# Modulation row tiles of the second layer and of the first gates, taken in pairs

## Chip, cores and metric

The kernel runs on one core of a Trainium2 chip. The metric is the device time of one execution in microseconds, median over runs.

## The reference, cut to what matters

Everything is float32 with 256 tokens of width 2048, a context of 256 more tokens, and two blocks after one another. The first block has two layers, each with a modulation that is worked out from a condition vector:

```python
cond, cond_ctx = silu(c), silu(c_ctx)
for i in range(2):
    shift, scale, gate = split(cond @ ada_w[i] + ada_b[i], 3)      # ada_w[i]: 2048 x 6144
    h  = rmsnorm(x, norm_g[i]) * (1 + scale) + shift
    shift_c, scale_c, gate_c = split(cond_ctx @ ada_w[i] + ada_b[i], 3)
    hc = rmsnorm(ctx, norm_g[i]) * (1 + scale_c) + shift_c
    # layer 0: sliding-window attention, 16 query heads of 128 in 4 groups, its gate and output product
    # layer 1: latent attention (MLA)
    x = x + gate * o
    ctx = ctx + gate_c * oc                                        # layer 0 only
```

Then the second block: pooling mixer, MLP (2048 to 8192 and back), dilated attention, MLP, each with a layer norm.

## The kernel before

**Weight tiles.** All weights come from one stream of tiles of 128 x 2048 float32 (1 MB). `Ring` (L99 on) gives each tile taken one of five slots, the one that was released first; SyncE (L1142 on) issues one transfer for each tile in this order and waits before each for the last use of the slot. A tile of a panel is "parted": ScalarE copies it to a rounded high part `whi` (L1170, three buffers), VectorE subtracts to give the low part `wlo` in place of the raw tile (L1663), and TensorE makes three products from the two. A row tile is not parted: `row_tile` (L608) runs 4 products of `condL` (32 columns) with the raw tile, at four column positions of the array, each as two float32 instructions, so 8 instructions a tile; four tiles (k = 0 to 3) make one row of 512 modulation values in PSUM bank 5 (bank 4 or 5 for gates). Their line is L614. The row is then copied by ScalarE to `arow`, and two blocks later `ada_cols` (L627) turns it into columns, which VectorE adds to the bias.

**When a tile may be parted.** At many places in TensorE's program a mark notes how far the ring stands. ScalarE and VectorE run the same marks in their own programs and part, at a mark, all tiles that it allows:

```python
def ahead(self, stand, look):                                                    # Ring, L139
    taken, now, kept = stand
    last = min(taken - 1 + look, len(self.order) - 1)
    ready = (n for n in range(last + 1) if self.before[n] is not None and self.done_at[self.before[n]] > now)
    return next(ready, last + 1) - 1, kept
```

`look` is 2 in the attention panels and the output panels. Row tiles count as places in the ring's order. The mark of a slot is made before the row tile of this slot; a row's fourth tile makes a further mark, which ScalarE uses when it copies the row (`row_kept`). The order of the parting is thereby fixed when the program is built, and each engine does its own work in program order.

**The stages that the change touches.** For i = 0 to 3 (four panel pairs) the query panel (blocks 0 to 15) and the gate panel (blocks 16 to 31) of the first layer run as 32 blocks; a block is 12 matmuls, a weight tile serves 4 blocks. After each block `swa_slot(i, blk)` (L746) runs: the mark, then the attention steps that `ATT_AT` places there, then a row tile if `(i, blk)` is in `ADA1_AT` (L214), then `ada_cols` if the row's last tile was two blocks ago. The steps of group g run in pair g + 1: in pairs 1 and 2 after blocks 0, 1, 3, 5, 6, 8, 10, 12, 13, 15, 17, 18, 20, 22, 24, 25, 27, 29, 31; in pair 3 group 2 after 0, 1, 2, 3, 5, 6, 7, 8, 10, 11, 12, 14, 15, 16, 17, 19, 20, 21, 23, and group 3 after each block from 24 to 31 and of the first output panel from 0 to 10. A step on TensorE is the scores of n (L728, bank 6), the transposes of the probabilities of n - 2 (L604, bank 4), the product with the values of n - 3 (L741, bank 7). VectorE reads the scores of n (L1833), then scales the probabilities of n - 1 (L1844); ScalarE takes the exponential of n (L1305), then copies the transposed n - 2. In pair 3 the gated output is prepared beside it: from block 20 on ScalarE makes a high part `og_hi` and VectorE a low part `og_lo` after each step.

The output panels (p = 0 to 3, 16 blocks each) have `out_slot(p, b)` (L772): mark, steps (p = 0), and a row tile of gate p where `GATE_AT` (L215) has b; at b = 14 the gate is spread over the partitions (`gate_rows`). Their block 12 needs the last of `og_lo`.

Of the kernel before, what the change touches and what calls it, by code (L numbers as in the profile page):

```python
# [50 lines left out]
def ada_tiles(layer, n):  # L51

    if layer == 0:
        return [4 * n + k for k in range(4)]
    return [88 + 16 * (n // 3) + 4 * k + 1 + n % 3 for k in range(4)]
# [155 lines left out]

ATT_AT = att_places()
Q3_TURN = (3, 23)
ADA1_AT = {(i, 4 * j + 1): (2 * i + j // 4, j % 4) for i in range(4) for j in range(8)}  # L214
GATE_AT = {1: 0, 4: 1, 8: 2, 11: 3}  # L215
KV_ORDER = [(n, k) for k in range(4) for n in range(2)]
ADA0_AT = [5, 2, 6, 3, 7]
ADA1_ORDER = [0, 4, 1, 5, 2, 6, 3, 7]
# [29 lines left out]
def program(nc, a, out):  # L248
    ring = Ring()
    psum = Banks(ring)  # L250
    with ExitStack() as ctx:
# [192 lines left out]
        def _(pe):  # L444
            mm, tr = nc.tensor.matmul, nc.tensor.transpose

            def open_bank(key, bank, parts=1):

                b, before = psum.take(key, bank, parts)
                need(pe, bank_free[b], before)  # L450
                if b in psum.beside:
                    first, n = psum.beside.pop(b)
                    pe.wait_ge(bank_free[first], n)
                return b
# [13 lines left out]
            def weight(T, parts=True):  # L468

                n = ring.take(T, parts)  # L470
                if parts:
                    pe.wait_ge(hi_done, ring.nth[n] + 1)
                else:
                    s, v = ring.landed(n)
                    pe.wait_ge(landed[s], v)
                return n
# [10 lines left out]
            def used(n, ins):  # L487

                ins.then_inc(tile_used, 1)
                tiles_used[0] += 1  # L490
                ring.used(n, (tile_used, tiles_used[0]))

            def used_with(n, key):

                b, v, _ = psum.at[key]
                ring.used(n, (bank_full[b], v))
# [111 lines left out]
            def row_tile(key, T, k, bank):  # L608

                if k == 0:  # L610
                    open_bank(key, bank)
                n = weight(T, parts=False)
                for c in range(4):
                    last = mm(PS[32 * c:32 * c + 32, bank, :], condL[:, 4 * k + c, :], raw[:, ring.place[n], c * PW:(c + 1) * PW],  # L614
                              start=(k == 0), stop=(k == 3), tile_position=(0, 32 * c))
                if k == 3:
                    psum.mark(key)
                    last.then_inc(bank_full[bank], 1)
                    used_with(n, key)
                else:  # L620
                    used(n, last)
# [5 lines left out]
            def ada_cols(layer, n, bank):  # L627

                given(("row", layer, n))
                key = ("cols", layer, n)  # L630
                b = open_bank(key, bank)
                for c in range(4):
                    last = mm(PS[:, b, 2 * c:2 * c + 2], arow[:, c * P:(c + 1) * P], selcol[:], start=True, stop=True)
                psum.mark(key)
                last.then_inc(bank_full[b], 1)

            def gate_rows(layer, s, bank, p, rows):

                pe.wait_ge(bias_in, 16 * (5 if layer else p + 1))
                given(("row", layer, 8 + p))  # L640
                b = open_bank(("gate", layer, s, p), bank)
                last = mm(PS[:, b, :], selrow[:, s, :], rows, start=True, stop=True)
                psum.mark(("gate", layer, s, p))
                last.then_inc(bank_full[b], 1)
# [38 lines left out]
            for m, (n, k) in enumerate(KV_ORDER):  # L683
                pe.wait_ge(h_ready, 4 * (k + 1))
                pe.wait_ge(hi_done, ring.nth[kv[m]] + 1)
                for t in range(4):
                    b = open_bank(("kv", n, k, t), t)
# [23 lines left out]
            def turn_heads(what, i, n):  # L711

                pe.wait_ge(qk_ready, n)
                for h in range(4):
                    turn((what, i, h), 4 + 2 * (h % 2), [QS[:, t, h * HD:(h + 1) * HD] for t in range(4)])


            def swa_step(g, n):
                if n < 16:
                    h, t = n // 4, n % 4  # L720
                    if n == 0:
                        given(("q", g, 2))
                        given(("q", g, 3))
                        for t_ in range(4 if g == 0 else 0):
                            given(("kv", 1, 3, t_))
                    b = open_bank(("s", g, n), 6)
                    keys = kT[:, g, 0:512] if t < TT else kT[:, g, 256:512]
                    last = mm(PS[:, b, 0:keys.shape[-1]], qT[:, h, t * P:(t + 1) * P], keys, start=True, stop=True)  # L728
                    psum.mark(("s", g, n))
                    last.then_inc(bank_full[b], 1)  # L730
                if 2 <= n < 18:
                    u = n - 2
                    pe.wait_ge(swa_p, 16 * g + u + 1)
                    turn(("p", g, u), 4, [Sb[:, u % 3, c * P:(c + 1) * P] for c in range(4 if u % 4 < TT else 2)])
                if 3 <= n:
                    u = n - 3
                    given(("p", g, u))
                    b = open_bank(("o", g, u), 7)
                    toks = range(4) if u % 4 < TT else range(TT, 4)
                    for c, t in enumerate(toks):  # L740
                        last = mm(PS[:, b, 0:P], V0[:, t, g * HD:(g + 1) * HD], PTb[:, u % 2, c, :],  # L741
                                  start=(c == 0), stop=(c == len(toks) - 1))
                    psum.mark(("o", g, u))
                    last.then_inc(bank_full[b], 1)

            def swa_slot(i, blk):  # L746

                psum.mark(("slot", i, blk))
                for g, n in ATT_AT.get((i, blk), ()):
                    swa_step(g, n)  # L750
                if (i, blk) == Q3_TURN:
                    turn_heads("q", 3, 20)
                if (i, blk) in ADA1_AT:
                    r, k = ADA1_AT[(i, blk)]
                    n = ADA1_ORDER[r]
                    row_tile(("row", 1, n), ada_tiles(1, n)[k], k, 5)
                if ADA1_AT.get((i, blk - 2), (0, 0))[1] == 3:
                    ada_cols(1, ADA1_ORDER[ADA1_AT[(i, blk - 2)][0]], 5)
                if i == 0 and blk == 11:
                    turn_heads("k", 0, 4)  # L760

            for i in range(4):
                rows_panel(("qp", i), swa_qg_tiles(i, 0), swa_x, (0, 1, 2, 3), slot=lambda b: swa_slot(i, b))
                cols_panel(("gp", i), swa_qg_tiles(i, 1), swa_xT, (0, 1, 2, 3), slot=lambda b: swa_slot(i, 16 + b))
                if i < 3:
                    turn_heads("q", i, 8 + 4 * i)
# [5 lines left out]
            def out_slot(p, b):  # L772

                psum.mark(("outslot", p, b))
                for g, n in ATT_AT.get((4, b), ()) if p == 0 else ():
                    swa_step(g, n)
                if b in GATE_AT:
                    row_tile(("row", 0, 8 + p), ada_tiles(0, 8 + p)[GATE_AT[b]], GATE_AT[b], 5 - p % 2)
                if b == 14:
                    for s in range(2):  # L780
                        gate_rows(0, s, 6 + s, p, gaterow[:])

            for p in range(4):
                rows_panel(("so", p), swa_out_tiles(p), og_x, (0, 1, 2, 3), slot=lambda b: out_slot(p, b),
                           before=lambda k: pe.wait_ge(og_ready, 4 * (k + 1)) if p == 0 else None)
# [377 lines left out]
        def _(act):  # L1163
# [86 lines left out]
            def row_kept(layer, n):  # L1250

                order = ADA1_ORDER if layer else [0, 4, 1] + ADA0_AT
                r = order.index(n)
                if r or layer:
                    b, v, _ = at[("cols", layer, order[r - 1]) if r else ("cols", 0, 7)]
                    act.wait_ge(bank_full[b], v)
                take(("row", layer, n), arow[:], whole)
# [38 lines left out]
            def head_kept(what, i, h, dst):  # L1296
                take((what, i, h), dst[:, h, :], whole)
# [18 lines left out]
            def swa_slot(i, blk):  # L1316
# [4 lines left out]
                if (i, blk) == Q3_TURN:  # L1321
                    for h in range(4):
                        head_kept("q", 3, h, qT)
                if ADA1_AT.get((i, blk), (0, 0))[1] == 3:
                    row_kept(1, ADA1_ORDER[ADA1_AT[(i, blk)][0]])
                if i == 0 and blk == 11:
# [1096 lines left out]
```

## Time and profile before

| | |
|---|---|
| median of 3 runs | 3592.66 us (3592.44 to 3600.66) |
| the profiled execution | time 3590.74 us, span 3588.9 us |
| TensorE busy | 3472.1 us, 97% of the span |
| VectorE, ScalarE busy | 1891.0 us (53%), 1443.8 us (40%) |
| row-tile instructions (L614) | 768 in all, 96 tiles, 103.9 us busy |
| attention panels, output panels | about 172 to 673 us, 673 to 890 us |

TensorE's busy time is that of overlapping instructions, each begun before the one before it has ended, so durations in a row don't add up; the distance between the starts of equal instructions does. A timeline merges neighbouring equal instructions to one row with their number.

### The profile page before, as it was taken

How to read it: one execution, taken by the hardware profiler on the slowest of the kernel's cores; microseconds unless marked ns; L12 is line 12 of the kernel's file. 1: busy time of each engine (PE TensorE's matmuls, PEld its weight loads, DVE VectorE, ACT ScalarE, POOL GpSimd, SP SyncE). 2: the span in 40 equal slices, each digit the busy share in tenths (PEclk: the TensorE clock that was granted, in tenths of full speed). 3: DMA queues.
4: the chain of work that ended last, by engine and by line, in shares of the span. 5: the costliest groups of instructions: out<-in, count | busy, mean ns of one | idle time of the engine just before them, and what ended most of it. 6: DMA issues, size and time to landing. Idle time of an engine off the chain costs nothing.

```text
span 3588.9 us, 43519 instructions
## 1 busy us (share of the span) xinstructions
PE 3472.1 (97%) x18351; PEld 2850.3 (79%) x18351; DVE 1891.0 (53%) x2640; ACT 1443.8 (40%) x1612; POOL 142.8 (4%) x82
## 2 busy tenths in 40 slices
PE   7999999999999999999999999999999899999997
PEld 4677777776877668878888888878997788888886
DVE  3544455533666645457544554464445675445545
ACT  4213333422554443535433443343434444334432
POOL 0000000000000000005000000040000050000000
PEclk9999999999999999999999999999999999999999
DMA  9543333354332265454555555545543455555553
GB/s 367 224 168 137 130 130 121 115 211 164 114 112 83 106 255 182 169 206 164 211 190 197 188 188 188 189 170 188 176 153 141 164 188 211 190 197 188 188 189 127
DMA packets 90782, 626.07 MB, mean 174 GB/s; under 512 B 10326, under 2 KB 11351, under 8 KB 17755
## 3 DMA queue, kind: packets, MB, share of 16 engines
q1 hardware_dynamic: 85472, 606.72, 46.8%
q10 hardware_dynamic: 5116, 16.57, 1.2%
q8 instruction: 145, 2.38, 0.3%
q14 instruction: 49, 0.40, 0.0%
HBM read 621.15 MB, written 2.10 MB: 174 GB/s over the span
## 4 chain that ended last, share of the span: by engine, by line
PE 92%; DVE 4%; ACT 2%; issue 1%; DMA 1%; SPq 0%; DVEq 0%; ACTq 0%
PE PS L583 16%; PE PS L512 14%; PE PS L513 14%; PE PS L518 14%; PE PS L589 8%; PE PS L539 4%; PE PS L532 4%; PE PS L533 4%; PE PS L614 2%; PE PS L604 2%; PE PS L741 1%; PE PS L728 1%; DVE wlo L1663 1%; DMA raw<-in_weights 1%; PE PS L884 1%
## 5 line engine op out<-in xcount | busy, mean ns | idle before, releaser
L1663 DVE TENSOR_TENSOR wlo<-raw,whi 128x2048 fp32r<-128x2048 f32 (+1 forms) x484 | 1109.4, 2295 | 1113.0 <-ACT whi L1170 1102.6
L1170 ACT ACTIVATE whi<-raw 128x2048 fp32r<-128x2048 f32 (+1 forms) x484 | 911.9, 1886 | 1072.2 <-PE PS L518 617.7
L583 PE MATMUL PS<-xm,whi 128*128 128x512 f32 x2432 | 671.0, 397 | 14.8 <-DVE xm L1679 14.3
L583 PEld LDWEIGHTS PS<-xm,whi 128*128 128x128 f32 x2432 | 418.5, 190 | 74.5 <-DVE xm L1679 9.6
L589 PEld LDWEIGHTS PS<-xm,wlo 128*128 128x128 f32 x2432 | 375.4, 190 | 52.3
L512 PE MATMUL PS<-whi,hid_hi 128*128 128x512 f32 x1024 | 398.7, 389 | 0.0
L513 PE MATMUL PS<-whi,hid_lo 128*128 128x512 f32 x1024 | 398.4, 389 | 0.0
L589 PE MATMUL PS<-xm,wlo 128*128 128x256 f32 x2432 | 388.6, 282 | 0.0
L518 PE MATMUL PS<-wlo,hid_hi 128*128 128x512 f32 x1024 | 273.7, 389 | 0.0
L518 PEld LDWEIGHTS PS<-wlo,hid_hi 128*128 128x128 f32 x1024 | 192.2, 188 | 40.0
L513 PEld LDWEIGHTS PS<-whi,hid_lo 128*128 128x128 f32 x1024 | 192.2, 188 | 39.7
L512 PEld LDWEIGHTS PS<-whi,hid_hi 128*128 128x128 f32 x1024 | 192.2, 188 | 39.7
L512 PE MATMUL PS<-whi,og_hi 128*128 128x512 f32 x384 | 155.1, 404 | 3.8 <-ACT QS L1347 2.8
L513 PE MATMUL PS<-whi,og_lo 128*128 128x512 f32 x384 | 150.3, 392 | 0.0
L1305 ACT ACTIVATE Sb<-Sb,nm,qsc 128x512 f32<-128x512 f32 (+1 forms) x64 | 45.3, 709 | 222.4 <-DVE nm L1836 222.4
L614 PE MATMUL PS<-raw,condL 128*32 128x512 f32 x768 | 103.9, 623 | 26.0 <-DMA raw<-in_weights 26.0
L2273 POOL TENSOR_SCALAR X<-X,hrs,nmr 128x512 f32<-128x512 f32 x24 | 45.8, 1909 | 1552.8 <-PE PS L589 1552.8
L512 PE MATMUL PS<-whi,h_hi 128*128 128x512 f32 x256 | 105.0, 410 | 0.0
L532 PE MATMUL PS<-h_hi,whi 128*128 128x512 f32 x256 | 104.2, 407 | 0.0
L518 PE MATMUL PS<-wlo,og_hi 128*128 128x512 f32 x384 | 103.8, 392 | 0.3 <-DVE wlo L1663 0.3
L513 PE MATMUL PS<-whi,h_lo 128*128 128x512 f32 x256 | 100.2, 392 | 0.0
L533 PE MATMUL PS<-h_lo,whi 128*128 128x512 f32 x256 | 100.1, 391 | 0.0
(336 smaller groups left out, 5093.5 us busy)
## 6 DMA issues: line engine op xcount, KB each, us to landing
raw<-in_weights SPq DMA_DIRECT2D x560, 1024.0 KB, 4.8
lnB<-in_ln ACTq DMA_DIRECT2D x4, 2048.0 KB, 9.4
raw<-in_weights SPq DMA_DIRECT2D x8, 768.0 KB, 4.1
X<-in_x SPq DMA_DIRECT2D x4, 1024.0 KB, 8.3
X<-in_x ACTq DMA_DIRECT2D x4, 1024.0 KB, 15.7
raw<-in_weights SPq DMA_DIRECT2D x8, 512.0 KB, 3.7
raw<-in_weights SPq DMA_DIRECT2D x4, 640.0 KB, 3.9
out_x<-X SPq DMA_DIRECT2D x4, 512.0 KB, 3.4
```

What stands on the lines that cost most here:

```text
L512: mm(o, xh, high_of(n, cols), start=(k == 0 and c == 0), stop=False)
L513: mm(o, xl, high_of(n, cols), start=False, stop=False)
L518: last = mm(o, xh, low_of(n, slice(c * w, (c + 1) * w)), start=False, stop=(end and c == nch - 1))
L532: mm(o, high_of(n, f), xh, start=(start and c == 0), stop=False, skip_group_check=True)
L533: mm(o, high_of(n, f), xl, start=False, stop=False, skip_group_check=True)
L539: last = mm(o, low_of(n, f), xh, start=False, stop=(end and c == 3), skip_group_check=True)
L583: mm(PS[:, b, :], high_of(n, f), x(4 * k + c).rearrange("p s t -> p (s t)"), start=(k == 0 and c == 0), stop=False, skip_group_check=True)
L589: last = mm(PS[:, b, 0:TOK], low_of(n, f), x(4 * k + c)[:, 0, :], start=False, stop=(end and c == 3), skip_group_check=True)
L604: last = tr(PS[0:rows, b, n * P:n * P + k], blk, ident[0:k, 0:k])
L614: last = mm(PS[32 * c:32 * c + 32, bank, :], condL[:, 4 * k + c, :], raw[:, ring.place[n], c * PW:(c + 1) * PW], start=(k == 0), stop=(k = ...
L1170: return f(dst, src, ACT.Copy)
L1663: v.tensor_tensor(wlo[:, ring.place[n], 0:w], raw[:, ring.place[n], 0:w], whi[:, m % NH, 0:w], ALU.subtract).then_inc(lo_done, 1)
```

## The change

The 32 row tiles of the second layer that run in the attention panels are taken two at a time, after blocks 1, 9, 17 and 25 in place of 1, 5, 9, ..., 29 of each panel pair; a row is thus complete at block 9 or 25 (before: 13 or 29), and its column step comes at block 11 or 27 (before: 15 or 31). The 16 row tiles of the first layer's gates are taken two at a time after blocks 2 and 9 of each output panel (before: one after each of 1, 4, 8 and 11). ScalarE and VectorE read the same tables, so their copies of rows and columns move with them.

```diff
-ADA1_AT = {(i, 4 * j + 1): (2 * i + j // 4, j % 4) for i in range(4) for j in range(8)}
-GATE_AT = {1: 0, 4: 1, 8: 2, 11: 3}
+ADA1_AT = {(i, 8 * j + 1): (2 * i + j // 2, 2 * (j % 2) + 1) for i in range(4) for j in range(4)}
+GATE_AT = {2: 1, 9: 3}
@@ swa_slot
-                    row_tile(("row", 1, n), ada_tiles(1, n)[k], k, 5)
+                    for x in (k - 1, k):
+                        row_tile(("row", 1, n), ada_tiles(1, n)[x], x, 5)
@@ out_slot
-                    row_tile(("row", 0, 8 + p), ada_tiles(0, 8 + p)[GATE_AT[b]], GATE_AT[b], 5 - p % 2)
+                    for x in (GATE_AT[b] - 1, GATE_AT[b]):
+                        row_tile(("row", 0, 8 + p), ada_tiles(0, 8 + p)[x], x, 5 - p % 2)
```

## Rows read from the trace of the kernel before

**Rows 1.** The page: span, the chain's share by engine, issue to landing

```profile
span 3588.9 us, 43519 instructions
PE 92%; DVE 4%; ACT 2%; issue 1%; DMA 1%; SPq 0%; DVEq 0%; ACTq 0%
raw<-in_weights SPq DMA_DIRECT2D x560, 1024.0 KB, 4.8
```

**Rows 2.** Waits of PE, 150 to 900 us: who for whom, us, times, longest

```profile
PE PS L512 <- ACT QS L1347: 2.8, 1, 2.8
...
PE PS L604 <- ACT PTb L1170: 0.3, 1, 0.3
```

**Rows 3.** Timeline of PE, output panel: start us, us, instruction, number

```profile
745.28 1.07 PE L518 MATMUL PS<-wlo,og_hi 128*128 128x512 f32 x4
746.28 1.07 PE L614 MATMUL PS<-raw,condL 128*32 128x512 f32 x8
...
749.23 1.07 PE L518 MATMUL PS<-wlo,og_hi 128*128 128x512 f32 x4
751.95 1.07 PE L518 MATMUL PS<-wlo,og_hi 128*128 128x512 f32 x4
```

**Rows 4.** Timeline of PE, pair 3: a step with a row tile, then without

```profile
551.92 1.07 PE L518 MATMUL PS<-wlo,h_hi 128*128 128x512 f32 x4
...
557.85 1.08 PE L518 MATMUL PS<-wlo,h_hi 128*128 128x512 f32 x4
...
574.69 1.07 PE L518 MATMUL PS<-wlo,h_hi 128*128 128x512 f32 x4
...
579.42 1.07 PE L518 MATMUL PS<-wlo,h_hi 128*128 128x512 f32 x4
```

**Rows 5.** Timeline of PE, MLA stage: two row tiles back to back

```profile
1249.00 1.92 PE L614 MATMUL PS<-raw,condL 128*32 128x512 f32 x16
```

**Rows 6.** Timeline of ACT, pair 3, blocks 25 to 28

```profile
643.73 0.82 ACT L1305 ACTIVATE Sb<-Sb,nm,qsc 128x512 f32<-128x512 f32 x1 [1.69 <-DVE nm L1836]
...
644.73 0.62 ACT L1170 ACTIVATE og_hi<-GT 128x512 fp32r<-128x512 f32 x1
...
652.18 1.90 ACT L1170 ACTIVATE whi<-raw 128x2048 fp32r<-128x2048 f32 x1
```

**Rows 7.** Timeline of DVE, pair 3, blocks 26 to 28

```profile
646.31 0.42 DVE L1833 CUSTOM_DVE_ANT_0 Sb<-PS,masks 128x256 f32<-128x256 f32 x1
...
654.11 2.29 DVE L1663 TENSOR_TENSOR wlo<-raw,whi 128x2048 fp32r<-128x2048 f32 x1 [1.11 <-ACT whi L1170]
```

**Rows 8.** Timeline of ACT, pair 3, step of block 1

```profile
539.39 0.82 ACT L1305 ACTIVATE Sb<-Sb,nm,qsc 128x512 f32<-128x512 f32 x1 [1.56 <-DVE nm L1836]
```

**Rows 9.** Timeline of PE, pair 3, scores of block 3

```profile
545.59 0.59 PE L728 MATMUL PS<-kT,qT 128*128 128x256 f32 x2
```

**Rows 10.** Timeline of PE, pair 3: row tile of block 25, scores of block 27

```profile
641.34 1.06 PE L614 MATMUL PS<-raw,condL 128*32 128x512 f32 x8
...
648.82 0.59 PE L728 MATMUL PS<-kT,qT 128*128 128x256 f32 x2
```

**Rows 11.** Windows: stretch, its us, PE PEld DVE ACT POOL busy, PEclk, DMA share, GB/s

```profile
672.00:676.00 4.00, 2.88 (x10) 2.31 (x11) 0.00 (x0) 3.99 (x6) 0.00 (x0) 0.80 0.01 5
676.00:680.00 4.00, 4.00 (x19) 2.95 (x18) 3.51 (x7) 1.72 (x3) 0.00 (x0) 0.77 0.01 4
1614.00:1624.00 10.00, 6.58 (x19) 4.93 (x20) 9.33 (x16) 8.35 (x17) 0.00 (x0) 0.53 0.01 2
```

**Rows 12.** Timeline of PE, pair 3, column step of block 31

```profile
669.40 0.95 PE L633 MATMUL PS<-selcol,arow 128*128 128x2 f32 x8
```

**Rows 13.** Timeline of DVE, first output panel, last low part of the attention output

```profile
726.13 0.69 DVE L1679 TENSOR_TENSOR og_lo<-GT,og_hi 128x512 fp32r<-128x512 f32 x1 [0.70 <-ACT og_hi L1170]
```

**Rows 14.** Timeline of PE, first output panel, value product of block 10

```profile
723.70 0.60 PE L741 MATMUL PS<-PTb,V 128*128 128x128 f32 x4
```

## Prediction

> **What bounds the kernel now.** I read the page first: the span, then the chain of work that ended last. TensorE (PE) carries 92% of that chain [rows 1], so a change counts by what it does to PE's own stream and to PE's waits. Next came the waits of PE in the stretch that holds the first layer's attention and its output panels (150 to 900 us): one wait there is above 2 us, 2.8 us at the end of the attention panels for ScalarE's last gate [rows 2]. So here PE is a gapless stream, and whatever leaves the stream comes off the time, unless a wait grows. Then I read the timelines of PE, ScalarE (ACT) and VectorE (DVE) there, to see how early weight tiles are split and how much room the attention steps leave.
>
> **Part 1, what pairing saves.** In an output panel the last four matmuls of neighbouring blocks start 2.72 us apart, and 3.95 us apart with a row tile between [rows 3]: a lone row tile costs 1.23 us. Behind an attention step it costs 5.93 - 4.73 = 1.20 us [rows 4]. The MLA stage already has two row tiles back to back: 16 instructions take 1.92 us against 1.07 us for 8 [rows 3, 5]. The second of a pair so costs 0.85 us; what it doesn't pay again is the way in and out of a 32-column shape. The change makes 16 pairs in the attention panels and 8 in the output panels, each moving one tile: 24 x (1.21 - 0.85) = 8.7 us less of PE. The bounds are no saving (if the MLA row flatters, since its neighbours are plain float32 matmuls on both sides) and 9.1 us; I take 8.7, as both single rows agree.
>
> The Trainium skill (TensorEngine Tiling (Array Packing), Key Properties) says that changing the tiling mode drains TensorE. It gives no price; the trace agrees in sign, with 1.2 us for a lone tile and 0.85 us for a second one. By that rule alone the kernel would be 8.7 us faster, and nothing would speak against the change.
>
> **Part 2, transfers.** No tile is added; two raw row tiles are asked for together and then none for eight blocks. A slot of the ring is released seven to nine blocks ahead of the tile that takes it, some 20 us or more at 2.72 us a block [rows 3], against 4.8 us from issue to landing [rows 1]. PE waits for no landing in this stretch today, and three transfers in a row (up to 14 us) still fit. Nothing, with 0 to 1 us as bounds; SP's queue is passed by nothing else.
>
> **Part 3, the split of weight tiles moves.** This is what the diff doesn't show. ACT and DVE may split (high part, low part) weight tiles up to two places ahead in the ring's order of the tile last taken. Today the order alternates, weight, row, weight, row, so each weight tile is allowed as soon as the one before it is taken: one split every four blocks, four blocks early. With two rows in between, the first weight tile behind them isn't allowed before the rows are taken, and then two are allowed at once. So every eight blocks ACT gets two copies of 1.90 us in a row [rows 6] and DVE two subtractions of 2.29 us (2.2 us of pitch) [rows 7], at blocks 2, 9 or 10, 18 and 25 or 26 of each panel pair, two blocks before need. PE never waits for the weights themselves (earliest margin 0.9 us, at block 4 of the first pair). But both engines take work in program order, so the softmax step behind the copies is late, and PE's next step needs its result and its bank. Where steps lie two blocks apart (pairs 1 and 2) I find at most 2.6 us of delay and room for it. Pair 3, with a step at nearly every block, has none:
>
> Block 3 of pair 3: ACT's exponential starts at 539.39 [rows 8] and is over by 540.5; copies to 544.3; DVE's subtractions to 546.95; only then does it read the scores of block 2, freeing the bank at 547.4 and giving probabilities at 548.7. PE wants the bank at 545.59 [rows 9] + 0.85 = 546.4 and the probabilities 0.4 us later. Stall 1.0 + 0.8 = 1.8 us (0 to 3).
>
> Block 20: the same doubling falls beside head normalisation. By the same sum DVE's step 19 is 2.4 us late and PE loses about 0.8 us; a 0.3 us wait at block 17 [rows 2] goes. Net 0.5 us (0 to 2.3, one subtraction).
>
> Block 27, the largest. ACT's step of block 25 is over by 643.7 (its exponential, today at 643.73, comes 1.1 us earlier without a subtraction ahead) [rows 6]. Behind it stand, in order, two copies (to 647.5), the row's copy out of PSUM (648.0), and the output high part of 0.62 us (648.6) [rows 6]. DVE waits for that one before its own low part (649.2), then two subtractions (653.7), and only then reads step 26's scores, which it read at 646.31 [rows 7]. The bank is free at 654.15, while PE asks at 648.82 + 0.85 = 649.7 [rows 10]: 4.5 us. Then PE's transposes wait until ACT has done step 26's exponential and the previous probabilities' copy, 1.2 us more. Stall 5.7 us (2 to 7).
>
> **Part 4, the clock.** After PE's 2.8 us wait the granted clock reads 0.80 and 0.77 for 8 us, the lower level of 1.2 GHz for part of it: 4 x 0.20 + 4 x 0.23 = 1.7 us lost [rows 11]. Between the norm's waits at 1614 us it reads 0.53 for 10 us, 4.7 us lost [rows 11]. For 4.5 us of idling at block 27 I take the nearer row in surroundings, 1.7 us (0 to 4.7); nothing for block 3, whose idling is in two short pieces.
>
> **Part 5, what else moves.** The column step of the last row (0.95 us busy, 0.8 us of pitch) runs today at block 31 [rows 12], in the shadow of the 2.8 us wait, since ACT's chain to the last gate starts before it. At block 27 it has no cover: +0.8 us, once; elsewhere it only changes place. In the first output panel, block 12 needs the last output rows; today their low part ends at 726.82 [rows 13] and the row tile at block 11 covers the chain from block 10's matmuls at 723.70 [rows 14]. That tile moves to block 9, and two subtractions now stand before the chain at block 10: some 1.1 us of stall (0 to 2.5). At block 3 of this panel the doubling just fits.
>
> **Sum.** -8.7 + 1.8 + 0.5 + 5.7 + 1.7 + 0.8 + 1.1 = +2.9 us. Against the profiled execution (span 3588.9 [rows 1], time 3590.74, so 1.84 us around the span) that is 3593.6; the median of the runs, 3592.66, is 1.9 us above it, so the forecast is 3595.6. A measurement of this kernel can tell about 0.3% (10.8 us) from no change.
>
> **Rivals.** (B) The delays are absorbed: ACT or DVE has more room than my hand sum gives, and only the column step stays. 3592.7 - 8.7 + 0.8 = 3584.8. For it: today's stretch of steps hides single splits with a 0.3 us wait as the worst [rows 2]. Against: two in a row are twice the delay, and the high part in the middle chains ACT to DVE. (C) The slower side, by the clock: if the idling at blocks 3 and 27 of pair 3 each puts PE at 1.2 GHz for 10 us as near 1614 us [rows 11], and the spell at 672 us lengthens likewise, then 2.9 - 1.7 + 9.4 + (4.7 - 1.7) = +13.6 us, 3606.3. It decides from whether these stalls grow past the 2.8 us that today costs 1.7. The Trainium skill (TensorE: Matmul & The Clock Gate, Part 1) says that idling brings the array to half clock and sustained work brings it back; the trace shows both levels, and only the size is open. (D) The pairing doesn't do what it says: a second tile costs like a lone one between weight blocks, and only the losses stay, 3592.7 + 11.6 = 3604.3. Against it stands the pitch of eight more instructions inside one group [rows 5].
>
> **How the numbers follow.** Forecast 0.55, B 0.25, C 0.10, D 0.06; 0.04 for a gain beyond B (a faster edge than any row shows). The forecast's own range, by its bounds, is 3589 to 3602. To leave out no more than 2 in 10 the whole range takes in B and ends below C and D: 3584 to 3603. Faster by over 0.3% (under 3581.9) 0.03, within 0.83, slower (over 3603.4) 0.14, from C, most of D, and the upper edge of the forecast left out.
>
> **What would show it.** Groups of 16 row-tile instructions at 1.9 us, 24 of them before 900 us; ACT's copies and DVE's subtractions in twos; PE waits for DVE's scores or probabilities near 546, 620 and most of all 650 us, with a lower clock behind the last; a longer wait for the last gate. If the waits near 650 us are missing, part 3 was wrong and B holds. If PE waits for a landing, part 2 was.

## The result, and the profile after

The changed kernel takes 3599.86 us (median of 12 runs, 3595.09 to 3608.10), beside 3592.55 us for the kernel before (12 runs, 3587.23 to 3600.66). The ratio is 1.0022, with a 95% interval of 1.0012 to 1.0031: some 8 us slower (4.3 to 11.1), and within the 0.3% that the prediction called no change. The forecast was 3595.6 us in a range of 3584 to 3603.

The page of the kernel after: span, share of the chain by engine, issue to landing (before: [rows 1]).

```profile
span 3602.2 us, 43501 instructions
PE 91%; DVE 5%; ACT 2%; issue 1%; DMA 1%; SPq 0%; DVEq 0%; ACTq 0%
raw<-in_weights SPq DMA_DIRECT2D x560, 1024.0 KB, 4.8
```

The profiled execution took 3604.03 us, and its span is 13.3 us above that of before. Nearly half of this lies ahead of anything that the change touches. The first matmul of the key and value weights starts at 59.30 us and not at 53.12, since the granted clock is low in the start-up of this execution. Two windows of 40 to 60 us, before and then after (stretch, its us, busy time of PE, PEld, DVE, ACT and POOL, granted clock, DMA share, GB/s):

```profile
40.00:60.00 20.00, 17.02 (x125) 11.58 (x126) 9.56 (x21) 11.81 (x20) 0.00 (x0) 1.00 1.01 412
```

```profile
40.00:60.00 20.00, 17.01 (x101) 14.08 (x102) 7.00 (x18) 12.03 (x19) 0.00 (x0) 0.72 0.74 301
```

The same kernel was profiled once more below, and there this matmul starts at 53.27 us. So spans of whole profiles aren't compared here, but the stretch from that matmul to the first transposes behind the first layer, after a wait of 10.40 us that every kernel has: 848.8 us before (53.12 to 901.90), 854.1 after (59.30 to 913.35), +5.3 us. Within it, the waits of PE from 150 to 910 us (who for whom, us, times, longest):

```profile
PE PS L728 <- DVE mx L1835: 4.6, 2, 4.0
PE PS L512 <- ACT QS L1349: 3.6, 1, 3.6
PE PS L604 <- ACT PTb L1172: 3.2, 3, 1.1
...
PE PS L512 <- DVE og_lo L1681: 0.8, 1, 0.8
```

Against [rows 2] the wait for the last gate (QS) has grown by 0.8 us; the waits for scores' readers (mx) and for `og_lo` are new; those for the probabilities (PTb) were one of 0.3 us. Where they stand, in the timeline of PE (start us, us, instruction, number, idle time before it and what ended it):

```profile
549.67 0.70 PE L728 MATMUL PS<-kT,qT 128*128 128x256 f32 x2 [0.60 <-DVE mx L1835]
551.46 0.63 PE L604 MATMUL PS<-ident,Sb 128*128 128x128 f32 x4 [1.09 <-ACT PTb L1172]
...
625.56 0.41 PE L604 MATMUL PS<-ident,Sb 128*128 128x128 f32 x2 [1.06 <-ACT PTb L1172]
...
658.15 0.70 PE L728 MATMUL PS<-kT,qT 128*128 128x256 f32 x2 [4.00 <-DVE mx L1835]
659.95 1.08 PE L604 MATMUL PS<-ident,Sb 128*128 128x128 f32 x4 [1.09 <-ACT PTb L1172]
...
741.39 0.50 PE L512 MATMUL PS<-whi,og_hi 128*128 128x512 f32 x1 [0.82 <-DVE og_lo L1681]
```

These are block 3, block 20 and block 27 of pair 3 and block 12 of the first output panel. The cause shows on ScalarE and VectorE ahead of block 27 (compare [rows 6] and [rows 7]):

```profile
647.92 3.70 ACT L1172 ACTIVATE whi<-raw 128x2048 fp32r<-128x2048 f32 x2
651.52 0.57 ACT L1172 ACTIVATE arow<-PS 128x512 f32<-128x512 f32 x1
652.00 0.62 ACT L1172 ACTIVATE og_hi<-GT 128x512 fp32r<-128x512 f32 x1
```

```profile
652.65 0.69 DVE L1681 TENSOR_TENSOR og_lo<-GT,og_hi 128x512 fp32r<-128x512 f32 x1 [4.98 <-ACT og_hi L1172]
653.26 4.49 DVE L1665 TENSOR_TENSOR wlo<-raw,whi 128x2048 fp32r<-128x2048 f32 x2
657.67 0.42 DVE L1835 CUSTOM_DVE_ANT_0 Sb<-PS,masks 128x256 f32<-128x256 f32 x1
```

Two copies in a row, the row's copy, the high part of the output; VectorE idles 4.98 us for that last one, subtracts twice, and only then reads the scores of the step. PE had asked at 658.15 - 4.00 = 654.15.

The saving shows in the output panels, timeline of PE:

```profile
811.00 1.07 PE L518 MATMUL PS<-wlo,og_hi 128*128 128x512 f32 x4
812.00 1.92 PE L614 MATMUL PS<-raw,condL 128*32 128x512 f32 x16
...
815.83 1.08 PE L518 MATMUL PS<-wlo,og_hi 128*128 128x512 f32 x4
818.56 1.07 PE L518 MATMUL PS<-wlo,og_hi 128*128 128x512 f32 x4
```

The pitch is 4.83 us with a pair and 2.73 without, so a pair costs 2.10 us, where two lone tiles cost 2 x 1.23 [rows 3]: some 0.35 us saved a pair, and 8.4 us by 24 if each saves as much (the ledger below comes to 7.5).

Last the clock behind the wait at block 27, windows as above:

```profile
656.00:660.00 4.00, 0.75 (x3) 0.38 (x4) 3.09 (x8) 1.56 (x5) 0.00 (x0) 0.85 0.54 229
660.00:664.00 4.00, 4.00 (x20) 4.00 (x20) 2.19 (x9) 2.20 (x6) 0.00 (x0) 0.50 0.02 6
664.00:668.00 4.00, 4.00 (x11) 3.21 (x11) 1.02 (x3) 0.00 (x0) 0.00 (x0) 0.50 0.00 0
668.00:672.00 4.00, 4.00 (x20) 3.02 (x19) 1.51 (x7) 0.53 (x1) 0.00 (x0) 0.87 0.00 0
```

The granted clock is at the lower of its two levels, 1.2 GHz, for two whole windows. Lost: 0.6 + 2.0 + 2.0 + 0.5 = 5.1 us, against 1.7 us behind the only such wait of before [rows 11]. Here the spell starts behind the wait at block 27; behind the 3.56 us wait for the last gate this execution has none.

### The profile page after: what moved, and what is told of

It reads as the page before. It is cut to its first block, busy times and chain, and to the rows that moved or that the text cites. A ratio compares the mean times of both kernels' runs of the same rounds, so it can differ in the third digit from the quotient of the medians.

```text
span 3602.2 us, 43501 instructions
## 1 busy us (share of the span) xinstructions
PE 3475.3 (96%) x18351; PEld 2861.9 (79%) x18351; DVE 1889.8 (52%) x2640; ACT 1444.9 (40%) x1612; POOL 142.8 (4%) x82
## 4 chain that ended last, share of the span: by engine, by line
PE 91%; DVE 5%; ACT 2%; issue 1%; DMA 1%; SPq 0%; DVEq 0%; ACTq 0%
PE PS L583 16%; PE PS L512 14%; PE PS L513 14%; PE PS L518 14%; PE PS L589 8%; PE PS L539 4%; PE PS L532 4%; PE PS L533 4%; PE PS L604 2%; PE PS L614 2%; DVE wlo L1665 2%; PE PS L741 1%; PE PS L728 1%; ACT whi L1172 1%; DMA raw<-in_weights 1%
```

## The experiments

"Idle" below is PE's idle time that the kernel has more than before in this stretch, from the rows of its waits. "Clock" is what windows of 4 us from 540 to 760 us lost (1 less the granted clock, by their length), less the 1.7 us of before.

**The changed kernel again.**

> The changed kernel as it is, beside the experiments on the same chip. Theory (pairing saves 8.7 us of PE, splits in twos cost 11.6 us or more): 3 to 8 us above the kernel before, with waits of PE for DVE's scores near 550 and 658 us (0.6 and 4.0 us) again. Rival (the whole difference in the traces is the start-up's clock, 6 us before the stage that the change touches): within 2 us of the kernel before.

Measured: 3599.56 us (11 runs), 1.0014 (1.0005 to 1.0023) of before. Every wait in the stretch has the length it had above, but the clock is low twice, behind the wait at block 27 and again at the end of the last gate's wait, where PE goes on at 682.99 us:

```profile
652.00:656.00 4.00, 1.68 (x7) 1.31 (x8) 2.73 (x9) 1.88 (x5) 0.00 (x0) 0.77 0.34 141
656.00:660.00 4.00, 4.00 (x19) 3.90 (x19) 2.21 (x12) 1.88 (x5) 0.00 (x0) 0.50 0.03 6
660.00:664.00 4.00, 4.00 (x10) 3.05 (x10) 0.44 (x1) 0.00 (x0) 0.00 (x0) 0.50 0.00 0
664.00:668.00 4.00, 4.00 (x21) 3.09 (x20) 1.80 (x8) 1.33 (x5) 0.00 (x0) 0.95 0.00 0
680.00:684.00 4.00, 1.01 (x3) 0.85 (x4) 0.69 (x1) 3.97 (x7) 0.00 (x0) 0.68 0.48 201
684.00:688.00 4.00, 4.00 (x11) 3.12 (x10) 0.00 (x0) 1.60 (x2) 0.00 (x0) 0.50 0.00 0
```

Together these lose 8.4 us (8.6 with a last window at 0.96), where the first profile lost 5.1, and the stretch is 857.7 us, not 854.1. So the waits are fixed by the program and the clock isn't: one profile tells the idle time and only one draw of what the clock adds.

**Pairs, with the split kept even.** The row tiles stay in pairs, and only the rule for splitting weight tiles changes: at most one split tile ahead, counted in weight tiles and not in places of the ring. This holds for the attention panels and the first output panel.

```diff
+        last = (kept[0] if kept else len(self.parted)) + NH - 1
+        if self.most is not None:
+            last = min(last, len(self.parted) - 1 + self.most)
...
+            ring.most, psum.look = 1, 5
```

> The changed kernel with row tiles in pairs, but the splits of weight tiles allowed one at a time again, one tile ahead of the one in use, in the attention panels and the first output panel. Theory: the waits near 550, 625 and 658 us and the one at the output panel's block 12 are gone, the wait for the last gate is still about 3.6 us, and the gain of the pairs is left: 8.7 - 0.8 = 7.9 us less than the kernel before, about 3585 us. Rival (a pair saves less between weight blocks than in the MLA stage): waits gone, but 0 to 4 us less than before only. Rival (the waits come from the pair itself, since PE's row products keep the bank or the step late): the waits stay.

Measured: 3589.04 us (11 runs), 0.9989 (0.9980 to 0.9997) of before, 4 us faster. The waits of PE, same stretch (lines shifted by the edit):

```profile
PE PS L516 <- ACT QS L1355: 3.6, 1, 3.6
...
PE PS L608 <- ACT PTb L1178: 1.1, 1, 1.1
```

The waits for the scores' reader and for `og_lo` are gone, and the time is some 10 us below the changed kernel's. The expectation of 7.9 us below the kernel before was missed all the same, since the interval (1.1 to 7.2 us) ends short of it: the pairs save less than was reckoned (ledger), and a wait was left that I hadn't expected. What stays is the column step's two places: 0.8 us more ahead of the last gate, and 1.1 us at block 17 where 0.3 stood.

**The split in twos, with single rows.** The kernel before, with its row tiles where they were, but allowed to split in the rhythm of the changed kernel.

```diff
+                ring.most = (0, 0, 2, 2, 1, 1, 1, 1)[blk % 8]
...
+            psum.look = 5
...
+                if p == 0:
+                    ring.most = (0, 0, 0, 2, 1, 1, 1, 1, 0, 0, 2, 1, 1, 1, 1, 1)[b]
...
+                if blk in (9, 25):
+                    part_to(*psum.ahead[("slot", i, blk + 1)])
```

> The kernel before with its row tiles alone as they were, but the splits in twos at the places where the changed kernel has them (blocks 2, 10, 18 and 25 or 26 of each pair, 3 and 10 of the first output panel). Theory: the losses without the gain, 8 to 13 us more than the kernel before: waits for DVE's scores near block 3 and block 27 of pair 3 of at least 1 and 4 us, less where a row tile's 1.2 us falls before the step. Rival (the waits need both pairs and twos): under 3 us more than before.

Measured: 3612.32 us (5 runs), 1.0052 (1.0038 to 1.0065), 18.7 us slower (13.7 to 23.3), more than the 8 to 13 us expected. Waits of PE:

```profile
PE PS L516 <- ACT QS L1358: 4.6, 1, 4.6
PE PS L732 <- DVE mx L1844: 4.4, 1, 4.4
PE PS L608 <- ACT PTb L1179: 3.1, 3, 1.9
PE PS L516 <- DVE og_lo L1690: 1.9, 1, 1.9
```

In pair 3 VectorE's subtractions come in twos at the places of the changed kernel (540.45, 573.05, 613.49 and 652.85 us); ScalarE's copies do so only at the second and the fourth, where at blocks 2 and 18 one of the two is made earlier. So the doubled split alone, with no pair of rows, makes waits at the same four places, though not of the same length: 0.64 us at block 3 (changed kernel 0.60 + 1.09), 1.92 at block 20 (1.06), 4.40 + 0.57 at block 27 (4.00 + 1.09), 1.88 at block 12 of the first output panel (0.82). The wait for the last gate is longer too, 4.57 us where the kernel before has 2.77; why wasn't looked into. Their sum, 10.9 us more idle time than before, isn't the whole: windows from 620 to 692 us lose 8.5 us to the clock, 6.8 more than before.

**The output's high part ahead of the copies.** In the changed kernel ScalarE makes `og_hi` of block 25 before it copies the row and the two weight tiles.

```diff
+                if (i, blk) == (3, 25):
+                    gated_high(OG_BESIDE[blk])
...
-                    if i == 3 and blk in OG_BESIDE:
+                    if i == 3 and blk in OG_BESIDE and blk != 25:
```

> The changed kernel, with one order turned on ACT: at block 25 of pair 3 the high part of the attention output comes before the two copies of weight tiles and the row's copy, so that DVE doesn't stand idle behind them. Theory: DVE starts its subtractions 2.5 to 3 us earlier, PE's 4.0 us wait at block 27 falls to 1 to 1.5 us, the 1.1 us wait for ACT behind it stays, and with less idling the granted clock stays up or is low for a shorter time: 3 to 6 us less than the changed kernel. Rival (DVE's two subtractions alone make the wait): no more than 1 us less.

The wait at block 27, 4.00 us above, falls to 1.12:

```profile
655.27 0.70 PE L728 MATMUL PS<-kT,qT 128*128 128x256 f32 x2 [1.12 <-DVE mx L1837]
```

That is the link the prediction named: VectorE's subtractions had stood behind `og_lo`, which stood behind ScalarE's copies. The time, 3600.17 us (11 runs, 3586.56 to 3606.00; 1.0015, 1.0005 to 1.0025), doesn't show it. The stretch is 849.5 us, 4.5 less than in the changed kernel's first profile, while this execution has other low stretches of the clock later on, in the MLA stage: the granted clock is 0.51 from 1250 to 1260 us and again from 1280 to 1290, where the changed kernel has 0.83 and 1.00. The mechanism is shown, the gain in time isn't.

**Idle time alone.** The kernel before, with six useless reductions on VectorE ahead of the step at block 26 of pair 3, so that PE waits there. Nothing else moves.

```diff
+            for _ in range(6 if (i, blk) == (3, 26) else 0):
+                C(v.tensor_reduce(waited[:], masks[:], AX, ALU.max))
```

> The kernel before with six useless reductions of the mask table (896 columns each, about 1 us) on VectorE ahead of its step at block 26 of pair 3, and nothing else: an idle of PE at block 27 like the changed kernel's, with single row tiles and single splits. Theory (idle time at this place costs clock on top of itself, about as much again): PE waits 3.5 to 5 us for DVE's scores and 0.5 to 1.2 us for ACT behind, and the time is 8 to 11 us above the kernel before. Rival (the lower clock comes from elsewhere and an idle costs only itself): 4 to 6 us above.

```profile
654.53 1.22 PE L728 MATMUL PS<-kT,qT 128*128 128x256 f32 x2 [4.22 <-DVE mx L1833]
656.32 1.09 PE L604 MATMUL PS<-ident,Sb 128*128 128x128 f32 x4 [0.57 <-ACT PTb L1170]
```

```profile
652.00:656.00 4.00, 1.22 (x2) 0.50 (x2) 3.38 (x9) 1.18 (x4) 0.00 (x0) 0.73 0.55 231
656.00:660.00 4.00, 3.68 (x15) 3.52 (x16) 2.19 (x9) 2.58 (x8) 0.00 (x0) 0.50 0.00 0
660.00:664.00 4.00, 4.00 (x18) 2.94 (x18) 2.86 (x2) 1.80 (x1) 0.00 (x0) 0.91 0.01 4
```

Measured: 3604.72 us (5 runs), 1.0034 (1.0021 to 1.0046), 12.2 us slower (7.5 to 16.5) for 4.8 us of idle time. The scores behind the wait take 1.22 us for two matmuls where [rows 9] shows 0.59, and the clock is at 0.50 for a whole window. Of the 5.1 us that the clock takes here beyond before, 3.4 lie behind this wait; the other 1.7 lie behind the wait for the last gate, which has its old length of 2.77 us but a low spell twice as long (0.65 and 0.50 from 680 to 688 us).

**Less idle time, and idle time elsewhere.** The same with four reductions, and with eight of them at block 11 of pair 3, where no other wait is near.

```diff
-            for _ in range(6 if (i, blk) == (3, 26) else 0):
+            for _ in range(4 if (i, blk) == (3, 26) else 0):
```

> As idle_27 with four reductions in place of six (4.45 us of VectorE in place of 6.68): PE waits about 2.0 us for DVE's scores at block 27 of pair 3 and 0.6 us for ACT. Theory (each us of idling in the dense stretch costs about one and a half more by the clock): 5 to 7 us above the kernel before. Rival (the clock only falls behind a single wait longer than some 3 us): 2 to 3.5 us above.

```profile
651.00 0.70 PE L728 MATMUL PS<-kT,qT 128*128 128x256 f32 x2 [1.96 <-DVE mx L1833]
652.79 0.63 PE L604 MATMUL PS<-ident,Sb 128*128 128x128 f32 x4 [1.09 <-ACT PTb L1170]
```

```diff
-            for _ in range(6 if (i, blk) == (3, 26) else 0):
+            for _ in range(8 if (i, blk) == (3, 11) else 0):
```

> As idle_27 with eight reductions ahead of the step at block 11 of pair 3, some 90 us ahead of the wait for the last gate: PE waits 3.5 to 4.5 us in two pieces at block 12. Theory (the place doesn't matter, idling does): 9 to 13 us above the kernel before, as idle_27. Rival (at block 27 the wait is dear because the wait for the last gate follows 28 us behind it): 4 to 7 us above.

```profile
594.81 1.22 PE L728 MATMUL PS<-kT,qT 128*128 128x256 f32 x2 [3.52 <-DVE mx L1833]
596.60 1.09 PE L604 MATMUL PS<-ident,Sb 128*128 128x128 f32 x4 [0.57 <-ACT PTb L1170]
```

Measured: 3598.19 us (1.0012, 1.0003 to 1.0020; 4.3 us slower) for 3.1 us of idle time, and 3599.50 us (1.0022, 1.0012 to 1.0032; 7.9 us slower) for 4.1 us. Neither median lies where its theory or its rival had put it, and neither interval tells the two apart. With the 12.2 us for 4.8 us of the run before, the medians are above the idle time each time and grow faster than it, but the intervals overlap, and that of the shortest (1.1 to 7.2) takes in the idle time alone. Block 11 isn't spared, so the low clock isn't a matter of the place near the end of the panels.

**Half of the change each.** Only the pairs of the attention panels, and only those of the output panels.

```diff
-ADA1_AT = {(i, 4 * j + 1): (2 * i + j // 4, j % 4) for i in range(4) for j in range(8)}
+ADA1_AT = {(i, 8 * j + 1): (2 * i + j // 2, 2 * (j % 2) + 1) for i in range(4) for j in range(4)}
...
```

> Only the attention panels' half of the change: their row tiles in pairs, the gates' row tiles one at a time. Theory: 16 pairs save 16 x 0.35 = 5.6 us; the waits at blocks 3, 20 and 27 of pair 3 (1.7, 1.1, 5.1 us), 0.8 us more before the last gate, and the clock behind the idling (about as much as the idling) stay: 7 to 11 us above the kernel before, a little above the changed kernel. Rival (the output panels carry half of the loss): under 5 us.

Measured: 3598.75 us (9 runs), 1.0021 (1.0012 to 1.0031), 7.5 us slower, with waits as after but for `og_lo`. In this execution the clock is low behind the two waits of block 3 too, which end at 543.90 and 545.69 us:

```profile
544.00:548.00 4.00, 2.91 (x15) 2.54 (x15) 2.08 (x11) 2.83 (x8) 0.00 (x0) 0.74 0.73 262
548.00:552.00 4.00, 4.00 (x17) 3.23 (x16) 0.29 (x1) 0.00 (x0) 0.00 (x0) 0.83 0.00 0
```

```diff
-GATE_AT = {1: 0, 4: 1, 8: 2, 11: 3}
+GATE_AT = {2: 1, 9: 3}
...
```

> Only the output panels' half of the change: the gates' row tiles in pairs, those of the attention panels one at a time. Theory: 8 pairs save 8 x 0.35 = 2.8 us, the wait for the last output rows at block 12 costs 0.8 us, the wait for the last gate is 2.8 us as before: 1.0 to 2.5 us less than the kernel before. Rival (twos in the first output panel cost as much as in pair 3): 1 to 4 us more.

Measured: 3596.48 us (11 runs), 1.0004 (0.9995 to 1.0013), 1.4 us slower (1.8 faster to 4.7 slower). The one new wait is that of block 12:

```profile
PE PS L512 <- DVE og_lo L1680: 0.8, 1, 0.8
```

Eight pairs save 2.8 us and this wait costs 0.8, so a gain of 2.0 us was due. The runs don't show it: 2.0 us faster lies just outside the interval, and by the ledger a pair saves less. The attention half carries the loss, by its waits and by the medians.

**Even split, and the column step back in its cover.** As the second experiment, with the column step six blocks after the row's last tile, which is at blocks 15 and 31 as before the change. VectorE's part moves in the same way.

```diff
-                if ADA1_AT.get((i, blk - 2), (0, 0))[1] == 3:
-                    ada_cols(1, ADA1_ORDER[ADA1_AT[(i, blk - 2)][0]], 5)
+                if ADA1_AT.get((i, blk - 6), (0, 0))[1] == 3:
+                    ada_cols(1, ADA1_ORDER[ADA1_AT[(i, blk - 6)][0]], 5)
```

> Pairs with even splits, and the column step put back to blocks 15 and 31, six blocks behind a row's last tile in place of two. Theory: at block 31 of pair 3 the step lies again in the shadow of the wait for the last gate (2.8 us in place of 3.6), and at block 15 its 0.8 us lies again ahead of the dense steps, where the 1.1 us wait for ACT falls to 0.3: 1.6 us less than with even splits alone, 5 to 6 us less than the kernel before. Rival (the 1.1 us wait comes from the pair's place, not from the column step): 0.8 us less only, the wait stays.

```profile
PE PS L516 <- ACT QS L1355: 2.8, 1, 2.8
...
PE PS L608 <- ACT PTb L1178: 0.3, 1, 0.3
```

Measured: 3586.01 us (11 runs), 0.9982 (0.9973 to 0.9991), 6.5 us faster than the kernel before (3.2 to 9.7), and 11.5 to 14.4 us faster than the changed one by the latter's two ratios. The waits are those of [rows 2] to the tenth, the pairs are kept, and the clock reads 1.00 from 540 to 760 us.

**The ledger.** Everything in us, against the kernel before, of which there is one profile; "pairs" is 0.35 us for each, the stretch is that of the profiled execution, the last column is the ratio of the runs.

| kernel | pairs | idle | clock | sum | stretch | runs |
|---|---|---|---|---|---|---|
| after | -8.4 | +9.2 | +3.4 | +4.2 | +5.3 | +7.9 |
| after, again | -8.4 | +9.2 | +6.9 | +7.7 | +8.9 | +5.0 |
| pairs, even split | -8.4 | +1.6 | 0 | -6.8 | -5.7 | -4.0 |
| and the column step back | -8.4 | 0 | -1.7 | -10.1 | -9.2 | -6.5 |
| split in twos, single rows | 0 | +10.9 | +6.8 | +17.7 | +16.3 | +18.7 |
| `og_hi` first | -8.4 | +6.3 | +1.7 | -0.4 | +0.7 | +5.4 |
| attention half | -5.6 | +8.3 | +1.7 | +4.4 | +5.6 | +7.5 |
| output half | -2.8 | +0.8 | 0 | -2.0 | +0.6 | +1.4 |
| idle time at block 27 | 0 | +4.8 | +5.1 | +9.9 | +9.8 | +12.2 |
| idle time at block 27, short | 0 | +3.1 | +3.4 | +6.5 | +6.2 | +4.3 |
| idle time at block 12 | 0 | +4.1 | +3.4 | +7.5 | +7.0 | +7.9 |

The sum meets the stretch within 1.5 us in all but the output half, which is 2.6 us longer. Three things make most of the differences, and the starts of the same matmuls in two traces show them. First, three executions have a low spell of the clock right behind the start of the stretch, ahead of what was edited. At the matmuls that start at 174.00 us in the trace before, the stretch is already 2.2 us longer in the output half, 1.1 in the changed kernel's second profile and 0.9 in the first run with idle time, and within 0.1 in the others.

Second, 24 pairs save 7.5 us and not 8.4. The kernel with the column step back has the waits of before, so its pairs can be read by themselves: over its attention panels it goes from 5.83 us late (179.82 for 174.00, the delay of its start-up) to 0.52 late (663.16 for 662.64), 5.3 us for 16 pairs, and over its output panels from 1.10 us early (680.28 for 681.38) to 3.34 early (877.16 for 880.50), 2.2 us for eight. With the 1.7 us of clock that the kernel before loses and this one doesn't, these make the whole 9.2 us. The two pairs of the first output panel save little, some 0.25 us together (1.35 us early at 729.92).

Third, "clock" also counts a low clock while PE stands idle, when it costs nothing: with the split in twos and single rows it is 0.58 from 684 to 687.35 us, all of it within the wait for the last gate. That is 1.4 us too much in the sum, as much as the stretch is short of it.

## Why the prediction was right

The sign of the forecast held, and the time lies inside its range; the size was too small (+2.9 us forecast, +7.9 measured, and 2.9 lies outside the interval of 4.3 to 11.1). The range was 19 us wide and took in the time of before as well, so it is the steps below and not the range that bear the prediction out. Nor is the forecast's own range, 3589 to 3602, the sum of the bounds that stand at its terms: they add up to 3586 to 3614. One term was clearly too small.

- **Part 1, the pairs.** 24 x 0.36 = 8.6 us (8.7 in the prediction) forecast from the MLA stage's two tiles back to back; 24 x 0.35 = 8.4 us by the pitch in the output panels, and 7.5 us when the matmuls of two traces are matched (ledger). The change does what it says, so rival D falls. The half that moves only output panels didn't resolve its own 2.8 us; the run with an even split and the column step back did resolve a gain, 6.5 us.
- **Part 2, transfers.** No new wait of PE for a landing, and 4.8 us from issue to landing as before.
- **Part 3, the split in twos.** Block 3: 1.8 us forecast, 0.60 + 1.09 = 1.7 measured. Block 20: 0.5 net forecast, 1.06 measured and the 0.3 us wait at block 17 gone, 0.8 net. Block 27: 4.5 + 1.2 = 5.7 forecast, 4.00 + 1.09 = 5.1 measured. The links there came as worked out too: in the prediction the high part of the output ends 1.1 us before PE asks (648.6 and 649.7), in the trace 1.5 us before (652.62 and 654.15), and VectorE reads the scores at 657.67, as its second subtraction ends. That the split is the cause and not the pairs is shown from both sides: without it these waits are gone (even split), and it alone makes waits at the same places (split in twos with single rows). So rival B falls: in pair 3 the delays weren't absorbed. In pairs 1 and 2 they were, as forecast.
- **Part 4, the clock. This is the term that was mis-sized.** The forecast took 1.7 us for the wait at block 27, from the one comparable spell [rows 11], and nothing for block 3. The two profiles of the changed kernel lose 3.4 and 6.9 us more than before, with no difference between their waits; the second is above the forecast's bound of 4.7 too. The zero for block 3 doesn't hold in every execution either: the attention half loses 1.7 us to the clock there, and the split in twos with single rows 1.7 us behind block 20. The row of before that I set aside as too far, 4.7 us near 1614 us, was nearer to the truth. With 5 us in place of 1.7, about the mean of the two profiles, the sum of the measured terms is -7.5 + 9.2 + 5 = +6.7 us, inside the interval. Part of why the forecast came no further off is that its idle time was a little too long (9.9 us, 9.2 measured), against pairs that were priced 1.2 us too high. The run with idle time alone shows that idle time costs more than its length with nothing else changed: 4.8 us of idle time, 12.2 us in all. Rival C had the right mechanism: behind block 27 both profiles lose 5.1 us, near its 4.7, and in the second the spell at the last gate is longer too, but none stands at block 3. Its price in all (9.4 us and 3.0) was too high, and its 13.6 us lies above the whole interval of the runs. The Trainium skill (TensorE: Matmul & The Clock Gate, Part 1) has idling bring the lower level and work bring it back; both levels show, and which of several waits gets the low clock differs between two executions of the same program.
- **Part 5.** The column step without its cover: 0.8 forecast, 3.56 - 2.8 = 0.8 measured, and it goes when the step is put back. Block 12 of the output panel: 1.1 forecast, 0.82 measured. What the prediction missed here is that the other place of the column step, block 15, costs too once the split is even: the wait at block 17 is then 1.1 us in place of 0.3, and moving the step back ends it. The prediction said that elsewhere the step only changes place. In the changed kernel itself there is no wait at block 17.

Several expectations of the experiments failed on size. Making `og_hi` first was to give 3 to 6 us; it took 2.9 us of idle time away, and the runs show no gain. The output half was to be 1.0 to 2.5 us faster; its runs can't tell it from the kernel before. The even split gave 4.0 us and not 7.9, the first run with idle time cost 12.2 us and not 8 to 11, the split in twos with single rows cost 18.7 and not 8 to 13, and the two last runs with idle time fell between theory and rival.

## What to carry to other kernels

A look-ahead that is counted in places of a queue changes its meaning when items of another kind are moved in that queue: here pairing row tiles saved 7.5 us, near what was meant, and cost 9.2 us of idle time, 8.4 of it because two splits were released at once. Count the look-ahead in the items that it is for, and leave covered work in its cover; both together made the same pairing worth 6.5 us. And price an idle time of the matmul engine above its length: in the three kernels with idle time alone the medians were 1.4, 1.9 and 2.5 times as much, and in the changed kernel, with the 7.5 us of the pairs set aside, 1.4 and 1.7 times.

## What the runs showed of the hardware

- The price of idle time in a dense stream of matmuls, with nothing else changed: 3.1 us cost 4.3 (1.1 to 7.2), 4.1 us cost 7.9 (4.3 to 11.5) and 4.8 us cost 12.2 (7.5 to 16.5). In the profiles of the last two, 3.4 us above the idle time are a granted clock down to 0.50 in the windows right behind it; for the first it is 1.7 us, and in the first and the third another 1.7 us fall behind the wait for the last gate, whose length is that of before.
- A spell of the low clock isn't tied to a wait of the program: the 3.56 us wait for the last gate had one at its end in one profile of the changed kernel (0.68 and 0.50 from 680 us; it begins before PE goes on at 682.99) and none in the other, though both have a spell behind block 27 that loses the same 5.1 us. With this wait at 2.77 us the spell took 1.7 us in the kernel before, 3.4 in the first run with idle time, and was absent with the column step back.
- Short waits can have one behind them: in the attention half 0.60 and 1.09 us of idle time at block 3, with 0.74 and 0.83 in the two windows there. In the changed kernel's own profiles the same two waits have none.
- The start-up has such spells too (0.72 from 40 to 60 us), worth 6.2 us at the first matmul of the key and value weights. Five of the twelve profiles have this one, among them that of idle time at block 12, where nothing of the change is in the program, and one of the changed kernel's two has not. A comparison of two profiles has to leave it out.
